# Moving the first output turns to a step's end, and scaling the latent keys by two broadcast products

## The reference

```python
a_q, a_k, a_v, b_b, b_c, b_x, c_q, c_kv, c_kr = split_in(h @ w_in)
q_c   = rmsnorm((rmsnorm(c_q, norm_qa) @ w_qb).reshape(B, T, 6, 96), qnorm_c)
ckv_n = rmsnorm(c_kv, norm_kva)
k_nope = (ckv_n @ w_kb).reshape(B, S, 6, 64);  v = (ckv_n @ w_vb).reshape(B, S, 6, 64)
k_c   = rmsnorm(concat([k_nope, broadcast(c_kr)], -1), knorm_c)     # 96 = 64 + 32 columns
q_c, k_c = rope on the last 32 columns, latent tokens only
o_a = rmsnorm(diff_attention(q_a, k_a, v_a), subln_a) * const       # 6 heads, two softmaxes each
o_c = softmax_attention(q_c, k_c, v_c)                              # 6 heads
y   = concat([o_a, b_b * conv3(b_c * b_x), o_c], -1) @ w_out
```

## Time and profile before

| | us |
|---|---|
| median of 3 runs (lowest, highest) | 2001.78 (2000.39, 2004.81) |
| profiled execution | 2002.92 |
| its span | 2000.9 |
| PE, DVE, ACT, POOL busy | 1843.9, 1407.7, 1029.8, 333.8 |
| latents of layer 0, layer 1 (about) | 167 to 207, 1060 to 1100 |
| steps from the first output turn to the last turns of the loop | 368.7 to 391.9, 1259.6 to 1282.8 |

### The profile page before, as it was taken

One profiled execution on the slowest core, in us unless ns is written; L12 is line 12 of the kernel. 1 busy time (PEld: TensorE's weight loads), 2 busy tenths in 40 slices (PEclk: granted clock), 3 DMA queues, 4 the chain that ended last, 5 costly groups with the idle time before them and its releaser, 6 DMA issues.

```text
span 2000.9 us, 28755 instructions
## 1 busy us (share of the span) xinstructions
PE 1843.9 (92%) x11276; PEld 1655.3 (83%) x11276; DVE 1407.7 (70%) x2014; ACT 1029.8 (51%) x1401; POOL 333.8 (17%) x507
## 2 busy tenths in 40 slices
PE   5999789799999999998997888897999999999994
PEld 3996777698999999998996776795788888888883
DVE  5487885547666566546477875446988888888887
ACT  4245686524211211124236776434777777777772
POOL 0083540111000000001084531100000000000002
PEclk8999799999999999999998899997999999999997
DMA  9225200023454444421230000007999999999995
GB/s 333 69 94 216 85 1 1 33 74 126 160 168 136 159 138 158 142 80 48 71 100 27 1 1 1 2 22 299 388 405 394 414 403 397 395 392 405 377 387 218
DMA packets 112439, 366.21 MB, mean 183 GB/s; under 512 B 7457, under 2 KB 65217, under 8 KB 85937
## 3 DMA queue, kind: packets, MB, share of 16 engines
q1 hardware_dynamic: 94448, 303.50, 40.5%
q0 software_dynamic: 13536, 48.39, 6.9%
q10 hardware_dynamic: 4320, 12.49, 1.6%
HBM read 349.23 MB, written 15.12 MB: 182 GB/s over the span
## 4 chain that ended last, share of the span: by engine, by line
PE 78%; DVE 9%; ACT 6%; DMA 3%; issue 2%; POOL 1%; SPq 0%; DVEq 0%; POOLq 0%; ACTq 0%
PE PS L2449 28%; PE PS L2338 26%; PE PS L2006 8%; PE PS L2393 5%; PE PS L2430 4%; PE PS L2094 3%; ACT E L909 3%; PE PS L2118 2%; DVE NM L1356 2%; PE PS L2129 2%; ACT PT L914 1%; DVE KCn L1303 1%; DMA araw<-in_w_ada_head 1%; DVE SS L1286 1%; DMA raw<-in_w_ada_head 1%
## 5 line engine op out<-in xcount | busy, mean ns | idle before, releaser
L2449 PEld LDWEIGHTS PS<-H,split 128*128 128x128 f32 x2304 | 339.0, 188 | 2.8 <-issue 1.7
L2449 PE MATMUL PS<-H,split 128*128 128x320 f32 x2304 | 340.7, 310 | 0.5 <-DVE H L1903 0.5
L1088 ACT CAST split<-raw 128x2048 fp32r<-128x2048 f32 (+2 forms) x64 | 112.8, 1763 | 225.9 <-PE PS L2449 174.3
L1550 DVE TENSOR_TENSOR msplit<-raw,msplit 128x2048 fp32r<-128x2048 f32 x82 | 187.9, 2292 | 36.7 <-ACT msplit L1045 36.6
L1639 DVE TENSOR_TENSOR split<-raw,split 128x2048 fp32r<-128x2048 f32 (+2 forms) x64 | 136.5, 2133 | 107.4 <-ACT split L1088 106.9
L1550 DVE TENSOR_TENSOR split<-raw,split 128x2048 fp32r<-128x2048 f32 x82 | 186.8, 2289 | 18.8 <-ACT split L1045 18.8
L2338 PE MATMUL PS<-split,HT 128*128 128x512 f32 x816 | 195.8, 396 | 2.8 <-DVE HT L1529 2.4
L1045 ACT CAST msplit<-raw 128x2048 fp32r<-128x2048 f32 x82 | 157.0, 1915 | 69.9 <-PE PS L2338 61.2
L2338 PE MATMUL PS<-msplit,HT 128*128 128x512 f32 x816 | 191.1, 390 | 1.6 <-DVE msplit L1550 1.6
L2338 PEld LDWEIGHTS PS<-msplit,HT 128*128 128x128 f32 x816 | 152.9, 188 | 34.1 <-DVE msplit L1550 2.4
L2338 PEld LDWEIGHTS PS<-split,HT 128*128 128x128 f32 x816 | 151.9, 189 | 34.1 <-DVE HT L1529 2.8
(11 more groups left out here) (350 smaller groups left out, 3090.9 us busy)
## 6 DMA issues: line engine op xcount, KB each, us to landing
raw<-in_moe_w_gate SPq DMA_DIRECT2D x55, 1024.0 KB, 7.6
raw<-in_moe_w_down SPq DMA_DIRECT2D x55, 1024.0 KB, 8.2
raw<-in_moe_w_up SPq DMA_DIRECT2D x54, 1024.0 KB, 7.5
DOTW<-in_w_ada_rows POOLq DMA_DIRECT2D x56, 512.0 KB, 4.0
raw<-in_w_ada_head SPq DMA_DIRECT2D x16, 1024.0 KB, 6.8
mraw<-in_moe_w_up SPq DMA_DIRECT2D x14, 1024.0 KB, 7.8
mraw<-in_moe_w_gate SPq DMA_DIRECT2D x13, 1024.0 KB, 7.4
mraw<-in_moe_w_down SPq DMA_DIRECT2D x13, 1024.0 KB, 8.4
```

The source lines that it names most:

```text
L1088: A.copy(split[u % 2][:, 0, 0:w], src[:, 0:w]).then_inc(S["split_hi"], 1)
L1550: V.tensor_tensor(msplit[n % M_SPLIT][:, 1, :], mraw[n % M_RAW], msplit[n % M_SPLIT][:, 0, :].bitcast(f32), ALU.subtract).then_inc(S["piec ...
L2449: ins = T.matmul(PS[:, 4 * (u % 2) + 2 * c + hf, 0:HALF], W[:, w, k, c * P:(c + 1) * P], A(a, k, hf), start=(k == 0 and w == 0 and a == 0) ...
```

## The change

Four edits, the same for both layers:

1. PE's `mix_turn` t moves from the start of step 53 + t to its end (behind the scores, the output product and the transposes of that step). ACT's `mix_hi` t moves from the start of step 53 + t to step 54 + t, behind the exponential and the copy of the transposed weights. DVE's `mix_lo` t moves from the end of step 53 + t to the end of step 54 + t. The convolution's high part moves from the start of step 58 to the end of step 52.
2. The keys are scaled by two broadcast products: all heads' 96 columns by the inverse roots (6 x 96 = 576 columns), then, after a wait for it, the last 32 columns of each head by their weights (6 x 32 = 192 columns). The weights of the first 64 columns of the keys are multiplied into the queries' weights once at the start (a score needs only their product).
3. In a latents pass ACT copies the turned group (`turn_out`) before it takes the root, and no longer after.
4. PE's query products of pass t wait for `lat_q` of pass t - 1 (their banks have been copied); only the key and value products still wait for `lat_k`. Before, both waited for `lat_k`.

```diff
 # mixer_act, latents
                 if t:
+                    turn_out(0, t - 1)
                     root(2 * HEADS, QK)
-                    turn_out(0, t - 1)
 # mixer_act, head loop
             for k in range(-2, ITEMS):
                 hg = groups_at(k, 0)
-                if 0 <= k - K_MIX < NT:
-                    mix_hi(k - K_MIX, 1, MIX_A, k - K_MIX)
-                if k == K_MIX + NT:
-                    A.copy(MIX[:, mix_slots(l, 0, MIX_CONV), :], CONV[:, :, :]).then_inc(S["conv_hi"], 1)
...
                     A.copy(PT[k % 2][:, 0:cols], PSF[:, 3072:3072 + cols]).then_inc(S["pt_out"], 1)
+                if 0 <= k - K_MIX - 1 < NT:
+                    mix_hi(k - K_MIX - 1, 1, MIX_A, k - K_MIX - 1)
                 if (hg := groups_at(k, 1)) is not None:
                     turn_out(*hg)
+                if k == K_MIX - 1:
+                    A.copy(MIX[:, mix_slots(l, 0, MIX_CONV), :], CONV[:, :, :]).then_inc(S["conv_hi"], 1)
 # mixer_dve
             def latents_scale(t, k, heads=range(HEADS)):
-                x, col = (KCn, G_KC) if k else (QC, G_QC)
                 first = 12 * (t % 2) + (HEADS if k and t < NT else 0)
-                for h in heads:
-                    ins = V.scalar_tensor_tensor(out=x[:, t, h, :], in0=x[:, t, h, :], scalar=RT[:, first + h:first + h + 1],
-                                                 in1=GR[:, l, col:col + QK], op0=ALU.mult, op1=ALU.mult)
+                if k:
+                    a, n = heads[0], len(heads)
+                    x = KCn[:, t, a:a + n, :]
+                    ch.then(V.tensor_tensor(x, x, RT[:, first + a:first + a + n].unsqueeze(2).broadcast_to([P, n, QK]),
+                                            ALU.mult))
+                    x = KCn[:, t, a:a + n, NOPE:QK]
+                    g = GR[:, l, G_KC + NOPE:G_KC + QK].unsqueeze(1).broadcast_to([P, n, ROPE_W])
+                    ins = V.tensor_tensor(x, x, g, ALU.mult)
+                else:
+                    ... (the queries as before)
-                if 0 <= k - K_MIX < NT:
-                    mix_lo(k - K_MIX, 1, MIX_A, k - K_MIX)
+                if 0 <= k - K_MIX - 1 < NT:
+                    mix_lo(k - K_MIX - 1, 1, MIX_A, k - K_MIX - 1)
 # lambdas, once at the start: the six scalings of gains are now chained by waits, and
+                    ins = V.tensor_tensor(GR[:, l, G_QC:G_QC + NOPE], GR[:, l, G_QC:G_QC + NOPE],
+                                          GR[:, l, G_KC:G_KC + NOPE], ALU.mult)
 # mixer_pe, latents
-                if t:
-                    pe.wait_ge(S["lat_k"], l * KT_TILES + t)
                 if t < NT:
+                    if t:
+                        pe.wait_ge(S["lat_q"], l * NT + t)
                     ... (query products)
+                if t:
+                    pe.wait_ge(S["lat_k"], l * KT_TILES + t)
 # mixer_pe, head loop: this block stood first in the step, now it stands last
+                if 0 <= k - K_MIX < NT:
+                    t = k - K_MIX
+                    if t == 0:
+                        pe.wait_ge(S["turn_out"], (l + 1) * TURNS)
+                    else:
+                        pe.wait_ge(S["mix_lo"], l * 10 + t)
+                    pe.wait_ge(S["subln_gained"], l * NT + t + 1)
+                    mix_turn(t, 1, QA[:, t, :])
```

More of the change, by code:

```diff
@@ L1299, in latents_scale @@
             def latents_scale(t, k, heads=range(HEADS)):
-                x, col = (KCn, G_KC) if k else (QC, G_QC)
                 first = 12 * (t % 2) + (HEADS if k and t < NT else 0)
-                for h in heads:
-                    ins = V.scalar_tensor_tensor(out=x[:, t, h, :], in0=x[:, t, h, :], scalar=RT[:, first + h:first + h + 1],
-                                                 in1=GR[:, l, col:col + QK], op0=ALU.mult, op1=ALU.mult)
+                if k:
[7 more added lines that the diff above has]
+                else:
+                    for h in heads:
+                        x = QC[:, t, h, :]
+                        ins = V.scalar_tensor_tensor(out=x, in0=x, scalar=RT[:, first + h:first + h + 1],
+                                                     in1=GR[:, l, G_QC:G_QC + QK], op0=ALU.mult, op1=ALU.mult)
                 if heads[-1] == HEADS - 1:
@@ L1652, in lambdas @@
                     for col, n, factor in ((G_QA, DA, DA ** -0.5), (G_SUB, VA_W, 1.0 - l_init), (G_QC, QK, QK ** -0.5)):
-                        V.tensor_scalar(GR[:, l, col:col + n], GR[:, l, col:col + n], float(factor), None, ALU.mult)
+                        ch.then(V.tensor_scalar(GR[:, l, col:col + n], GR[:, l, col:col + n], float(factor), None,
+                                                ALU.mult))
+                    ins = V.tensor_tensor(GR[:, l, G_QC:G_QC + NOPE], GR[:, l, G_QC:G_QC + NOPE],
+                                          GR[:, l, G_KC:G_KC + NOPE], ALU.mult)
+                    ch.then(ins)
                 dve.wait_ge(S["lam_exp"], 1)
@@ L2136, in mixer_pe @@
             for k in range(-2, ITEMS + 1):
[L2137 to L2144, removed]
                 if k + 2 < ITEMS:
```

## The result

The changed kernel takes 2018.47 us (median of four runs, 2012.27 to 2021.30), the kernel before in the same session 2003.04 (2000.39 to 2004.81): ratio 1.0074, 95% interval 1.0057 to 1.0091, some 15 us slower. A second set gave 2020.72 against 2001.76, ratio 1.0083 (1.0063 to 1.0102). The sign was forecast, the size was not: +6.8 forecast, +15 to +19 measured. Both medians lie above the range.

A forecast was written before the change was run, and what follows sets the result against it. It took dense PE products to hold most of the chain, with PE, DVE and ACT cycling at the head loop's end. Latents -2.2 and -1.6, small pieces +0.4, turns +7.0, clock +3.2: +6.8, 2008.6 us; range 2003 to 2017.

The forecast's parts named there:

- The latents, 3.8 us: Latents stages: key scaling and earlier copy of the last keys save 2.2 us in layer 1, 1.6 in layer 0.
- the sum: Whole kernel: all terms added, -2.2 - 1.6 + 0.4 + 7.0 + 3.2 = +6.8 us.
- The turns, +3.5 a layer: End of each head loop: turns wait in a longer cycle through PE, DVE and ACT; +3.5 us a layer, +7.0 in all.
- rings of 4.7, 5.1, 5.5 and 4.4 us: End of the head loop: four successive waiting cycles from turn to turn, 4.7 to 5.5 us each, against 3.7 before.
- the convolution's copy at 0.5: End of the head loop: moving this copy earlier would alone give 0.5 us, but vanishes under the turns' cycle.
- The clock, +1.6 a layer: End of the head loop: PE's clock falls at about 1276 behind an idle gap; +1.6 us a layer, 3.2 in all.
- the third gap: Third cycle of turns: PE idles 3.3 us in one piece, and the clock is expected to fall there.
- stays low until the output projection: Rival: clock stays low until the output projection is under way; 12 us in place of 3.2, +15.6, 2017.4; 10%.

The follow-up runs named there:

- E2: Kernel before with only the turns' edits (PE's turn, high and low parts, convolution's copy); 2022.8 us, ratio 1.0102.
- E12: Kernel before with only PE's waits split by use and ACT's turned copy ahead of the root; 2001.7 us, ratio 0.9998.
- repeat: Changed kernel unaltered, measured and profiled again in the second set; 2020.7 us, ratio 1.0083.
- E6: Changed kernel with 44 idle transposes a layer ahead of PE's waits for turns 1 to 4; 2007.8 us, ratio 1.0026.
- E7: Kernel before with the latents' edits and the convolution's copy moved to step 53, turns in their old place; 2002.1 us, ratio 1.0002.
- E10: Changed kernel with ACT's high part between the exponential and the transposed copy; 2005.9 us, ratio 1.0009.
- E13: Changed kernel, high part ahead of the exponential, idle transposes at layer 1's waits, including 10 ahead of its first query product; 1995.2 us, ratio 0.9967.
- E9: Kernel before, old latents, with the turns' edits but the high part ahead of the exponential; 2000.3 us, ratio 0.9986.
- E3: Changed kernel with ACT's high part put back to the next step's start, ahead of the exponential; 1998.6 us, ratio 0.9975.
- E4: Changed kernel with the high part ahead of the exponential and DVE's low part ahead of the maximum; 2007.3 us, ratio 1.0018.
- E11: Changed kernel, high part ahead of the exponential, idle transposes at PE's waits in layer 1's latents and ahead of its first scores; 1997.2 us, ratio 0.9961.
- E1: Kernel before with only the latents' edits, turns in their old places; 2001.5 us, ratio 0.9992.
- E8: Kernel before with only the two broadcast scaling products and their weights; 2006.9 us, ratio 1.0023.

## Why the prediction was right and wrong

**The latents, 3.8 us: right as a piece, and not kept.** The table makes a square for layer 1. Old scaling without a fall at the first query product 37.1 to 37.2 (before, E2, E12), new scaling without 35.2 (repeat, E6, E7, E10, E13); old with that fall 39.4 (E9), new with it 37.5 (after, E3, E4, E11; 36.8 in E1 and E8, where it lasts 4 us and not 7). So the edit gives 1.9 to 2.0 us there where 2.2 was forecast, and a fall at the first query product costs 2.3. But in nine of eleven profiles the head loop behind takes it back. In layer 0 the latents gave 1.9 for 1.6, by another way than forecast: the sum had ACT's turned copy out of the way and PE's late load holding the rest, but E12 shows the moved copy and the split waits to be worth nothing, and the load came 1.9 us earlier. In a median the latents' edits gained nothing: E1 has -0.2 us where the sum has -3.4. That the clock can take back what shorter passes give was no term of it.

**The turns, +3.5 a layer: right, 3.4 by E6,** by the members named. Forecast were rings of 4.7, 5.1, 5.5 and 4.4 us; E6, with the clock held, has 4.8, 5.0, 5.5 and 4.5. The 6.0 of the fourth ring in the first profile is the clock's. I put the convolution's copy at 0.5 where it is 0.2.

**The clock, +1.6 a layer: the step that failed.** In the first profile this term was right in place and size: the fall came behind the third gap, at 1280.1, which by the table load is 1276.7 on the time of the kernel before (forecast about 1276), and it cost 1.56 a layer (47.67 - 46.11), all of it in the fourth ring, as the working had it. That this execution was the one profiled first is luck. In the common run the clock costs 5.2 to 6.3 a layer. In layer 1 of the repeat it falls again behind the fourth ring's own gap, with last turns and output projection behind it; in layer 0 of the repeat and in both layers of E2, whose ends last 50.49 and 51.73, it falls already behind the second gap, of 2.6 us. That was my rival "stays low until the output projection", +12 in place of 3.2 by the prediction's own working; I gave it 10%, and these profiles show it to be the common case. By its arithmetic it stood at 2017.4, and 2018.5 was measured; part of that closeness is luck, as the rival kept the latents' gain, which didn't come. I weighed one gap at a time, where four follow each other. The old loop's even 1.00 was taken as a sign of robustness.

**What is left.** The rings' 6.8 and the clock's 11.5 (6.3 + 5.2) make +18.3; with the -0.2 that E1 measured for the latents' edits +18.1. Measured are 15 to 19. E6, with the clock held at both ends, would be 6.8 - 0.2 = 6.6 over before, and is 6.0. So the 9 to 12 us that the forecast lacks are the clock in the ends, 8.3 (11.5 for 3.2), and the latents' gain of 3.4. The second part is seen in the profiles, as in E6's head loop of layer 1 (140.9 for 138.2); what makes that loop's low stretch longer is not shown.

## What to carry to other kernels

Before a wait of the main engine is moved to a step's end, write down which of its own later work the released instruction stands behind on every other engine: a copy that was in the shade becomes a member of a ring by standing behind one exponential. Price each microsecond of ring twice, once as itself and once as a part of a gap behind which the matmul clock may fall, and count all the gaps of the row, not the widest one. Measure a gain over many runs and between the same two instructions, and then again to the end of the next stage: here a piece that got 1.9 us shorter in its own stretch was mostly gone at the end of the head loop.

## What was not expected of the hardware

Useless work made the kernel faster: 88 idle transposes in gaps gave 13 us (2020.7 to 2007.8). The time of one and the same program differs by how the clock's low stretches fall: E1's runs spread over 12 us (1995 to 2007) at mean granted clocks of 0.965 to 0.973, the changed kernel's over 13 (2011.3 to 2024.3) at 0.957 to 0.969, and in both the longer runs are mostly those at the lower clock. What a low stretch costs depends on where it lies: in layer 1's latents and head loop E11's 20 us more at the higher level bought 0.5 us against E3, but 6.8 us of low clock later in the head loop goes with about 2 us (138.1 to 139.2 for 136.1 to 136.4).
